# Hybrid layer on one core: the first projection slab loaded ahead of six of the eight conditioning slabs, five of its nine tiles multiplied in four passes, token loads first

## What is computed

```python
mod = jax.nn.silu(c) @ ada_w[l] + ada_b[l]          # c_ctx for the context tile
sh1, sc1, g1, sh2, sc2, g2 = jnp.split(mod, 6, axis=-1)
h = rmsnorm(x, norm1_g) * (1 + sc1) + sh1            # modulate()
mq, mk, mv, mo, mi, mf, sz, sxbc, sdt, nq, nk, nv = project(h, w_in)
# an mLSTM, a state-space mixer and a neighbourhood attention read the projections;
# their outputs go through w_out, then a top-k mixture of 16 experts, then a last rmsnorm
```

## Time and profile before

| | before |
|---|---|
| time, median of 3 runs | 1687.42 us (1686.66 to 1687.46) |
| the profiled execution's own time | 1689.6 us |
| its span in the trace | 1687.9 us |
| TensorE busy | 1625.5 us, 96% of the span |
| VectorE, ScalarE, GpSimd busy | 42%, 23%, 21% |
| first projection matmul starts | 46.90 us |

### The profile page before, as it was taken

How to read it: one execution, slowest core, us unless ns; L and a number is a source line. 1 busy time by engine, 2 the same in 40 slices (tenths; PEclk the granted TensorE clock), 3 DMA queues, 4 the chain that set the end, 5 groups by cost and what they waited for, 6 DMA issues and landing times. The chain is left out here.

```text
span 1687.9 us, 28355 instructions
## 1 busy us (share of the span) xinstructions
PE 1625.5 (96%) x11310; PEld 1415.4 (84%) x11310; DVE 701.6 (42%) x1778; ACT 395.3 (23%) x954; POOL 356.5 (21%) x427
## 2 busy tenths in 40 slices
PE   5999999999999899999989999999999999999997
PEld 3876876666668566788879999999999999999994
DVE  4001047775655788222363322333332233333225
ACT  5220113341212466211131111111111111111113
POOL 2000000015322633121112112222211222221111
PEclk9999999999999899999999999999999999999999
DMA  8411112132212666322179988988888888888862
GB/s 314 138 52 53 59 36 60 46 112 35 52 34 94 204 173 215 114 94 94 52 286 362 322 276 271 312 272 295 312 287 288 273 301 282 280 314 290 295 212 113
DMA packets 213486, 323.75 MB, mean 192 GB/s; under 512 B 29680, under 2 KB 102377, under 8 KB 213371
## 3 DMA queue, kind: packets, MB, share of 16 engines
q1 hardware_dynamic: 180731, 282.66, 47.7%
q0 software_dynamic: 8560, 16.39, 5.1%
q10 hardware_dynamic: 24080, 23.02, 4.9%
HBM read 293.85 MB, written 24.99 MB: 189 GB/s over the span
## 5 line engine op out<-in xcount | busy, mean ns | idle before, releaser
L1805 PE MATMUL psum<-arena 128*128 128x144 f32 x4096 | 505.8, 286 | 1.7 <-DVE arena L2414 1.7
L1805 PEld LDWEIGHTS psum<-arena 128*128 128x128 f32 x4096 | 502.7, 190 | 2.8 <-ACT arena L1255 1.9
L1815 PE MATMUL psum<-arena 128*128 128x144 f32 x2048 | 253.5, 286 | 0.0
L1815 PEld LDWEIGHTS psum<-arena 128*128 128x128 f32 x2048 | 251.8, 190 | 0.0
L1403 PE MATMUL psum<-arena 128*128 128x384 f32 x720 | 243.1, 493 | 0.0
L2457 DVE TENSOR_TENSOR arena<-gt,psum 128x144 f32<-128x144 f32 x128 | 39.0, 304 | 443.3 <-PE psum L1805 402.1
L852 POOL DMA_INDIRECT expert_list<-gt x128 | 125.9, 983 | 457.0 <-DVE gt L2443 412.4
L1403 PEld LDWEIGHTS psum<-arena 128*128 128x128 f32 x720 | 134.6, 191 | 90.2 <-issue 3.1
L1406 PE MATMUL psum<-arena 128*128 128x256 f32 (+2 forms) x864 | 166.0, 353 | 1.2 <-DMA arena<-in_w_in 1.2
L1406 PEld LDWEIGHTS psum<-arena 128*128 128x128 f32 x864 | 146.1, 192 | 19.4 <-issue 1.7
L2327 DVE SCALAR_TENSOR_TENSOR arena<-arena,gt 128x1024 f32<-128x1024 f32 x128 | 159.0, 1279 | 0.7 <-DMA arena<-affinity_rows 0.7
(11 more groups left out here) (346 smaller groups left out, 1643.8 us busy)
## 6 DMA issues: line engine op xcount, KB each, us to landing
arena<-in_exp_w SPq DMA_DIRECT2D x96, 2048.0 KB, 9.5
arena<-in_ada_w SPq DMA_DIRECT2D x24, 1024.0 KB, 6.9
arena<-in_w_in SPq DMA_DIRECT2D x11, 1024.0 KB, 5.6
arena<-in_x_sample SPq DMA_DIRECT2D x16, 512.0 KB, 4.4
arena<-affinity_rows SPq DMA_DIRECT2D x16, 512.0 KB
arena<-m_decay_rows ACTq DMA_DIRECT2D x36, 128.0 KB, 3.3
arena<-decay_rows ACTq DMA_DIRECT2D x24, 192.0 KB, 3.5
out<-arena SPq DMA_DIRECT2D x9, 512.0 KB
```

The source lines that it names most:

```text
L1805: ins = mm(bank[:, 0:SLOTS], w[:, k, col], xeT[:, k, :], start=(k == 0), stop=(k == KD - 1))
L1815: ins = mm(bk[4 + db % 2][:, 0:SLOTS], wslot[4 + db // 4][:, k, (db % 4) * P:(db % 4) * P + P], hid[:, k, :], start=(k == 0), stop=(k == K ...
```

## The change

- **Slab order.** The z slab becomes slab 2, behind two conditioning slabs. It stays in ring place 2 until z is finished, and the conditioning slabs 3 to 9 use only the three other places (`None` entries are skipped by `load_slab`). The other projection slabs follow.
- **z in passes.** Five of z's nine token tiles are multiplied in four passes (`z_pass(j, tiles)`): pass j handles channel blocks 2j and 2j+1 of the five tiles, accumulating in five PSUM banks (0, 4, 5, 6, 7), as soon as those two blocks of `hT` are scaled. Between the pieces of pass j stand the products and picks of the conditioning pair j+1. The remaining four tiles of z run as before.
- **Loads.** Token tiles are issued first on SyncE, then the five rows of `smalls`; the nine loads of `vecs` move to ScalarE's DMA queue. TensorE turns the vectors after tile 0's transposes.
- **Norm.** Scaling and power of a tile's sum both go to GpSimd, tile by tile (`x_rstd`), ahead of its big memsets; VectorE's `x_norm` is tile by tile. ScalarE alternates one square with one copy of a transposed tile.
- **ScalarE's scaling before its rows.** In each pair, ScalarE scales its channel block first and copies the next two product rows after.

```diff
-    return [ada[m] for m in MODS1] + win1 + win2 + [None, None] + ada[8:] + wout
+    a = [ada[m] for m in MODS1]
+    return (a[:2] + win1[:1] + a[2:5] + [None] + a[5:] + [None] + win1[1:4] + [None, None]
+            + win1[4:] + win2 + [None, None] + ada[8:] + wout)
...
+        Z_BANK = (0, 4, 5, 6, 7)
+        NZ = len(Z_BANK)
...
# SyncE
-            for dst, src, rows in ((V_C, c_ctx, 8), ...
-                sp.dma_start(vecs[dst:dst + rows, :], ...).then_inc(vecs_in, 16)
+            for i in range(NT):
+                sp.dma_start(X[:, i, :], ...).then_inc(rows_in[i], 16)
             for dst, src, n in ((R_FB, f_bias, 8), ...
                 sp.dma_start(smalls[:, dst:dst + n], ...).then_inc(vecs_in, 16)
-            for s in range(8 + RING):
+            for s in range(14):
                 load_slab(s)
...
# GpSimd
+            def x_rstd(i):
+                pool.wait_ge(sumsq_done, i + 1)
+                one = rstd[:, 0, i:i + 1]
+                pool.tensor_scalar(one, sumsq[:, 0, i:i + 1], 1.0 / D, EPS, ALU.mult, ALU.add).then_inc(msq_done, 1)
+                pool.wait_ge(msq_done, i + 1)
+                pool.tensor_tensor(one, one, half[:, 0:1], ALU.pow).then_inc(rstd_done, 1)
+            for i in range(NT):
+                x_rstd(i)
             pool.memset(gt[:], 0.0)
...
# ScalarE
+            act.wait_ge(consts_ready, 1)
+            nc.scalar.activation(mrow[:, 0, 0:1], half[:, 0:1], ACT.Silu)
+            for dst, src, rows in ((V_C, c_ctx, 8), ...
+                act.dma_start(vecs[dst:dst + rows, :], ...).then_inc(vecs_in, 16)
...
-            for i in range(6):
+            x_square(0)
+            x_square(1)
+            for i in range(2, NT):
                 x_square(i)
+                x_turned(i - 2)
+                if i == 2:
+                    act.wait_ge(vcol_done, 1)
+                    nc.scalar.activation(scol[:], vcol[:, V_C:V_C + 16], ACT.Silu).then_inc(scol_done, 1)
...
# TensorE
+            def z_pass(j, tiles):
+                pe.wait_ge(xt_dve, NT + j + 1)
+                pe.wait_ge(xt_act, NT + j + 1)
+                for i in tiles:
+                    for k in (2 * j, 2 * j + 1):
+                        ins = mm(pj_bank(i)[:, 0:256], hT[:, k, i * P:i * P + P], ring[:, 2, k, 0:256],
+                                 start=(k == 0), stop=(k == KD - 1))
+                    if j == 3:
+                        ins.then_inc(pj_full, 1)
+            for i in range(6):
+                x_turn(i)
+                if i == 0:
+                    vectors_turned()
+            pe.wait_ge(cond_done, 2)
+            product(0)
+            x_turn(6)
+            x_turn(7)
+            pick_row(0)
+            product(1)
+            x_turn(8)
+            pick_row(1)
+            pe.wait_ge(vcol_done, 2)
+            slab_ready(2)
+            product(2)
+            for j in range(3):
+                z_pass(j, range(0, 2))
+                pick_row(2 * j + 2)
+                product(2 * j + 3)
+                z_pass(j, range(2, 4))
+                pick_row(2 * j + 3)
+                if j < 2:
+                    product(2 * j + 4)
+                z_pass(j, range(4, NZ))
+            z_pass(3, range(NZ))
...
-            for n in range(n_early):
+            for n in range(NZ, n_early):
```

More of the change, by code:

```diff
@@ L422, in hybrid_layer @@
         last_read = {}
-        for m, s in enumerate(list(range(8)) + list(range(G1, G1 + 16))):
+        for m, s in enumerate(A_S + list(range(G1, G1 + 16))):
             last_read[s] = (mod_full, m + 1)
@@ L433, in loads_of_slot @@
         def loads_of_slot(s):
-            return s // RING + (0 if s >= G1 and s % RING in ((G1 - 2) % RING, (G1 - 1) % RING) else 1)
+            return sum(slabs[t] is not None for t in range(s % RING, s + 1, RING))
+        Z_BANK = (0, 4, 5, 6, 7)
+        NZ = len(Z_BANK)
         def pj_bank(q):
+            if q < NZ:
+                return bk[Z_BANK[q]]
             if q < pe_index[n_early]:
-                return bk[4 + q % 4]
+                return bk[4 + (q - NZ) % 4]
             return bk[3 + (q - pe_index[n_early]) % 3]
         def pj_bank_before(q):
-            for first, banks in ((pe_index[n_early], 3), (0, 4)):
-                if q >= first:
-                    return q - banks if q - banks >= first else None
+            if q < NZ or pe_index[n_early] <= q < pe_index[n_early] + 3:
+                return None
+            return q - 4 if q < pe_index[n_early] else q - 3
         def first_visits(u):
@@ L499, in _, with load_slab @@
         def _(sp):
[L500 to L503, removed]
+            def load_slab(s):
+                if slabs[s] is None:
+                    return
+                mat, a, n = slabs[s]
+                read = [t for t in range(s % RING, s, RING) if t in last_read]
+                if read:
+                    sp.wait_ge(*last_read[read[-1]])
+                sp.dma_start(ring[:, s % RING, :, 0:n], w_src[mat][:, :, a:a + n]).then_inc(slab_in[s % RING], 16)
+            for i in range(NT):
+                sp.dma_start(X[:, i, :], x_prompt if i == 0 else x_sample[(i - 1) * P:i * P, :]).then_inc(rows_in[i], 16)
             for dst, src, n in ((R_FB, f_bias, 8), (R_DTB, dt_bias, 12), (R_ALOG, a_log, 12), (R_D, d_skip, 6),
@@ L1312, in slab_ready @@
                 pe.wait_ge(slab_in[s % RING], 16 * loads_of_slot(s))
[L1314 to L1338, removed]
@@ new lines, in product, with pick_row @@
+            def product(m):
+                slab_ready(A_S[m])
+                if m >= 2:
+                    pe.wait_ge(mrow_full, m - 1)
+                for k in range(KD):
+                    q = k % 4
+                    ins = mm(bk[1 + m % 2][32 * q:32 * q + 32, 0:SLAB], scol32[:, k, :], ring[:, A_S[m] % RING, k, :],
+                             start=(k < 4), stop=(k >= 4), tile_position=(0, 32 * q))
+                ins.then_inc(mod_full, 1)
+            def pick_row(m):
+                pe.wait_ge(mrow_full, m + 1)
+                if m >= 1:
+                    pe.wait_ge(modT_done, m)
+                for b in range(2):
+                    ins = mm(bk[3][:, 2 * b:2 * b + 2], mrow[:, m % 2, b * P:b * P + P], pick[:], start=True, stop=True)
+                ins.then_inc(modT_full, 1)
@@ L1354, in x_turn @@
                 ins.then_inc(xt_full, 1)
-            def x_turns(m):
-                if m is not None and m < 3:
-                    for i in range(3 * m, 3 * m + 3):
-                        x_turn(i)
-            mods(range(8), 0, x_turns)
+            def z_pass(j, tiles):
[32 more added lines that the diff above has]
+            z_pass(3, range(NZ))
             def group(n):
```

133 lines of the change are left out of this document (56 added, 77 removed).

## The result

| | before | after |
|---|---|---|
| time, median (13 runs each, alternating) | 1687.46 us (1686.66 to 1690.08) | 1691.06 us (1687.46 to 1694.32) |
| ratio, with its 95% interval | | 1.0018 (1.0011 to 1.0025) |
| the profiled execution, its span | 1689.6, 1687.9 us | 1693.56, 1691.8 us |
| tile 4 of z is multiplied | 66.7 us | 70.8 us |
| tile 5 of z is evacuated | 70.19 us | 74.46 us |

The change made the kernel 3.6 us slower, where 2.9 us faster was forecast. The span grew by 3.9 us, and tile 5 of z is evacuated 4.3 us later: the loss lies ahead of that point. (The 66.7 us is an evacuation, as in the prediction.

A forecast was written before the change was run, and what follows sets the result against it. TensorE's work list bounds the kernel once projections start. First scaled pair at 36.0, three rounds 23.5 and last pass 4.3 end tile 4 at 63.8 against 66.7: gain 2.9, 1684.5 us, range 1681.0 to 1688.6.

The forecast's parts named there:

- What was costed at nothing: List of zero-cost items: slab arrivals, bunched evacuations, SyncE's later loads, GpSimd's memsets, nine DMA issues on ScalarE.
- I take it that it stays up: TensorE's clock around the first scaled pair: stays at full speed, winning back 2.6 us of the old start.
- my first rival: Around the first scaled pair the clock falls, 2.6 us is paid again: gain 0.3, 1687.1 us; chance 0.22.
- Small rows queue behind the tokens: At the start, `smalls` loads wait behind nine token tiles in one queue; vectors complete at 15.5 us (14.7 to 16.0).
- The pace of 1.65 us: After tile 5's transposes, ScalarE sets each token tile's round: one square of 1.05 and one copy of 0.60.
- its three rounds: ScalarE's rounds after tile 5's transposes end at 25.7: three at 1.65 us give 30.7 for tile 7.
- The rounds: In z's passes, from one scaled pair to the next: 7.65 us plus 0.2 for TensorE's restart; three take 23.5.
- The last pass: End of z's passes: five tiles' matmuls after the last scaled pair, 4.3 us.
- the whole sum: Start to the end of z's tile 4: 36.0 + 23.5 + 4.3 = 63.8 us against 66.7, gain 2.9.
- The clock stays at 1.2 GHz through the passes: Rival in z's passes: one slow round cancels the gain, two make it 1692.7 us; chance 0.08.
- The small vectors did queue: Opposing rival at the start: small vectors do not queue, arrive about 8 us; gain 6.6, 1680.8 us; chance 0.13.
- nothing was given back later: Opposing rival after the projections start: VectorE's gate work or slab arrivals return the gain, 1687.4 us; chance 0.07.

The follow-up runs named there:

- the first experiment: The changed kernel with GpSimd's three big memsets moved between the power of tile 2 and that of tile 3: 1686.22 us, 0.9989 of the kernel before.

## Why the prediction was wrong

**The step that failed** stands under "What was costed at nothing": "GpSimd's large memsets now follow nine small scalings; what waits for them is the first evacuation, at about 60." I asked who waits for the memsets' results, and not who shares something with them while they run. Nobody waits for the results, but VectorE's scaling of tile 8 ran beside them: 5.52 us and not 0.75. Shown by three sides: away when the memsets move, away when another engine does the work, and made in the old kernel by moving one memset. The step bears 4.8 us at its place and, with the clock that it brought down, 6.1 us of tile 4's end (70.8 - 64.7).

The Trainium skill has this rule ("SBUF — State Buffer", Who interferes with whom): VectorE's copies and scalings from SBUF to SBUF can take a second pair of ports that is GpSimd's too, as an exclusive lock, and whoever comes second is blocked until the first one's instruction is over. The trace agrees, and goes further: the scaling was held not for the rest of one memset but over all three, 5.5 us. The section says also that ScalarE never waits on anyone; its 1.15 us beside the memset agree.

**The clock.** "I take it that it stays up" was wrong too. It fell in the hold, for 13.7 us (32.0 to 45.7), and made the first round 10.14 us and not 7.77: 2.4 us. Even without the hold it fell around the first pair, for 3.4 us, and cost the first piece 1.45 us (3.42 to 1.97). That is the mechanism of my first rival at about half its price; in the one execution that was traced, filling TensorE's two short waits there kept it up, so they are what brings it down. Filling only the long hold did not. The prediction also called the fall at 45 us "the one fall in the trace"; the kernel before has five more, at 232.4, 573.8, 584.0, 788.8 and 863.9 us.

**What was right.** Small rows queue behind the tokens: 15.48 for 15.5. In ScalarE's queue the last one was there at 10.27 (the kernel before with the loads alone) and at 11.8 (memsets early); at 12.70 (memsets first) TensorE came to the vectors without a wait. Tile 5 was turned by 25.6 for 25.7, though the clock rose at 21.8 and not 24.7. The pace of 1.65 us: tile 7 was turned 3.3 us later, by 28.9. The prediction has it at 30.7, but its three rounds end with tile 8, not with tile 7, and for tile 8 the sum came out (31.6 in the first experiment for 32.0). The rounds: 7.77 for 7.85, and where the clock stayed up throughout, three of them from the first pass to the last took 23.3 us (55.47 - 32.16) for 23.5. The last pass 4.4 for 4.3. No pass waited for a slab; the evacuations in a bunch cost nothing. With the memsets moved the whole sum came out nearly: tile 4 at 64.71 for 63.8, gain 1.95 for 2.9. There the first pair was 0.6 us early and the first round, at the low clock for a part, 1.4 us late; the two misses offset each other in part, which is luck.

**The rivals.** "The clock stays at 1.2 GHz through the passes" named the sign and nearly the time (1692.7), with a chance of 0.08, and its point of decision, about 12 us of low clock, was even reached. But its place was wrong: the passes themselves ran at full clock from 45.7 on, and what it lacked is the hold. That its time came near is luck. The small vectors did queue, and nothing was given back later: tile 5 is 4.3 us late, and the whole span 3.9.

**What stays open.** Times and traces up to tile 5 do not always agree: the kernel with tile 8 on ScalarE is 2.1 us slower than its trace says, the one with memsets early and small rows moved 1.9 us (0.3 of them outside the span), and five others are off by 0.8 to 1.4 us, to either side. The kept traces place the first of these. Against the first experiment it is 0.4 us late at 787 us, 1.2 us ahead at 821 us and 2.3 us late at 919 us (the same scaling on VectorE at 918.65 and 920.97). In between, the clock is low from 786.6 to 790.0, 844.6 to 848.0 and 854.8 to 858.3 us, and in the first experiment from 786.0 to 792.9 and 861.1 to 864.5: the same 10.2 us in all, at other work. In executions of one kernel the time goes with the mean granted clock (tile 8 on ScalarE: 1687.14 us at 0.990, 1691.39 at 0.988; correlation -0.90 over ten). So the place of the later falls is the likely cause, but no experiment moved them. Nor do the runs settle why the long hold, once filled, only put the clock's fall off.

## What to carry to other kernels

Work that nobody waits for is not free: before moving a large memset of GpSimd, look what VectorE does from SBUF to SBUF in the same microseconds, and put the memset where VectorE idles, at the start here. Look for such a hold as a maximum far above the median of one source line, since it hides in busy time and no wait is shown. A change of several parts can hide a good part behind a bad one: here the passes were worth some 13 us against the same kernel without them, and one misplaced trio of memsets cost 5.

## What the runs showed of the hardware

- One VectorE scaling was held through several GpSimd memsets in a row (2.76 + 0.96 + 1.37 us), though there is a boundary between each two; in another kernel it got in ahead of the third. What decides this is not shown.
- The hold goes both ways: GpSimd's scaling of a single column takes 0.19 us, but 0.62 and 0.75 beside VectorE's scaling of a tile, and the memset of `Hst` 1.92 and not 1.38.
- A row of some bytes, issued behind 4.5 MB of tokens in the same queue, lands with them: its waiter went on at 15.48 us, against 11.78 with the row in the other queue; it was issued at 6.92 and at 6.7.
- Two waits of TensorE of about 1 and 1.4 us among small matmuls were enough for 3.4 us of 1.2 GHz, in the one traced execution; with both filled the clock stood at 2.4 GHz there until 227 us.
